# A two-layer diffusion trunk with grouped experts: the order in which experts are worked, and where the loops over their blocks end

## The chip, the core and the metric

The kernel runs on one core of one Trainium2 chip. The core has five engines: TensorE (PE in the profile, PEld for its weight loads), VectorE (DVE), ScalarE (ACT), GpSimd (POOL) and SyncE (SP), which here only issues transfers. Sixteen DMA engines move data between the device memory (HBM) and the on-chip memory. The metric is the device time of one execution in microseconds (us), the median of three runs.

## The reference, cut to what matters

The network has two layers: a Conformer convolution layer and a gated-linear-attention layer, each followed by a mixture of experts. Only the mixtures matter here. There are 32 experts in 4 groups of 8; each token picks a group, then the 2 best experts in it:

```
g_idx = jnp.argmax(hf @ wg + bg, axis=-1)
inner = (hf @ wr + br).reshape(t, MOE_GROUPS, MOE_PER_GROUP)     # of the chosen group
top_v, top_i = lax.top_k(inner, MOE_TOP_K)                       # 2 of 8
top_w = jax.nn.softmax(top_v, axis=-1) * g_w
expert = g_idx[:, None] * MOE_PER_GROUP + top_i
y = (jax.nn.silu(xb @ w1[e]) * (xb @ w3[e])) @ w2[e]             # xb: the tokens of expert e
out[token] += y * weight
```

The width is 1024, the inner width 512. The first mixture sees 1280 tokens (256 of the context, 1024 latent), the second 1024. Everything is float32: w1, w3 and w2 of one expert are 2 MB each, 6 MB together (6 transfers of 1024 KB), and 32 experts make 201 MB a layer.

## The kernel before, in words

Each layer ends in two phases. **route** (from line 1056) takes the router's scores and works out, on DVE, which expert has how many tokens, in which order the experts are worked, and where each token's row goes. An expert's tokens are cut into *blocks* of 32 (`BLK`), and `need` is its number of blocks, at least 1. `place` is an expert's place in the order, 0 to 31. The results are small tables: `plan.order` (the expert at each place), `plan.ends` (blocks up to and with that place), `plan.block` (the count of all blocks) and `plan.token` (the rows of each block).

**experts** (from line 1408) then works the blocks in that order. Its engines run five programs that meet at semaphores:

- SP (lines 1456 to 1483) streams the weights. `feed.w` holds four experts (`BUFS`). The first three places always belong to experts 0, 8 and 16, whose weights are asked for already during route. For each place x, SP waits until the weights of x have landed and says so (`pair_ready` for w1 and w3, line 1467; `back_ready` for w2, line 1469). Then, while x+3 exists, it waits until place x-1 has left its buffer (`pair_done`, `back_done`) and issues the load of place x+3: four transfers of 1024 KB for w1 and w3 (line 1026) and two for w2 (line 1034). All this is one program in order: what it says of place x+1 is said after the load of x+3 has been issued.
- PE (lines 1515 to 1577): per block, `in_product` (line 1533, 32 weight loads and 32 matmuls of 32 tokens by 2 x 128 columns), the turn of the next block's tokens (line 1520), `out_product` of the block before (line 1526) and the turn of its activations (line 1548). A new place waits for `pair_ready` before its first block.
- ACT and DVE: the activation, the gate product, and copying results out of PSUM. ACT stores a block's 128 KB of results. After all blocks each has a `tail` for the last block's results, which PE writes to `py_last`.
- POOL gathers the 128 KB of tokens of a block four blocks ahead and, in the second layer, starts the final gathers when the last results are stored.

ACT, DVE and POOL share the loop in `blocks` (lines 1437 to 1450): four blocks written out, then a loop of four blocks a turn whose number of turns is that of the greatest possible count `nb` (112 blocks in the first layer, 96 in the second), and each block inside stands under `If(k < count)`. PE's own loops end at `plan.ends`.

Of the kernel before, what the change touches and what calls it, by code (L numbers as in the profile page):

```python
# [10 lines left out]
ALU = mybir.AluOpType  # L11
AX = mybir.AxisListType
ds = bass.ds

P = 128
# [12 lines left out]
GROUPS, PER_GROUP, EXPERTS, FF, BLK = 4, 8, 32, 512, 32  # L28
EXPERT_ORDER = [g * PER_GROUP + e for e in range(PER_GROUP) for g in range(GROUPS)]
AHEAD_X = 4  # L30
MIDDLE = 18
ROUND = float(1 << 23)
LAT, CTX = 0, 1
SH1, SC1, G1, SH2, SC2, G2 = range(6)
# [13 lines left out]
class Phase:  # L48
# [9 lines left out]
    def sb(self, name, shape, dt=F32):  # L58
        return self.ctx.enter_context(self.nc.sbuf_tensor(f"{self.name}_{name}", shape, dt))
# [31 lines left out]
def chain(ph, eng, name):  # L91

    done = [0]

    def link(ins):
        done[0] += 1
        ins.then_inc(ph.sem(name), 1)
        eng.wait_ge(ph.sem(name), done[0])
    return link
# [956 lines left out]
def route(nc, d, layer, streams, plan, lg, ranks, feed):  # L1056
# [4 lines left out]
    nb = plan.blocks  # L1061
    width = GROUPS + EXPERTS
    with ExitStack() as ctx:
        ph = Phase(nc, ctx, f"route{layer}")
        s = ph.sem
        sb = feed.room()
# [21 lines left out]
        need = sb([P, EXPERTS])  # L1088
        key = sb([P, EXPERTS])
        place = sb([P, EXPERTS])  # L1090
        bend = sb([P, EXPERTS])
        first_of = sb([P, EXPERTS])
        last_of = sb([P, EXPERTS])
        versus = sb([P, EXPERTS, EXPERTS])
# [7 lines left out]
        with nc.Block() as block:  # L1102
# [33 lines left out]
            def _(dve):  # L1136
                link = chain(ph, dve, "step")
# [70 lines left out]
                link(dve.tensor_tensor(versus, other(key), this(key), ALU.is_gt))  # L1208
                link(dve.tensor_reduce(key, versus, AX.X, ALU.add))
                link(dve.tensor_scalar(place, key, float(feed.AHEAD), 0.0, ALU.subtract, ALU.max))  # L1210
                link(dve.tensor_scalar(bend, key, -4.0, float(4 * MIDDLE - 3), ALU.mult, ALU.add))
                link(dve.scalar_tensor_tensor(place, bend, 0.0, place, ALU.min, ALU.add))
                link(dve.tensor_tensor(place, place, key, ALU.add))

                link(dve.tensor_tensor(versus, other(place), this(place), ALU.is_lt))
                link(dve.tensor_tensor(versus, versus, other(need), ALU.mult))
# [13 lines left out]
                for j in range(2):  # L1230
# [13 lines left out]
                by_place = inner_rows[0:1, :, :]  # L1244
# [7 lines left out]
                link(dve.tensor_tensor(by_place.rearrange("p x (e g) -> p x e g", g=GROUPS),  # L1252
                                       versus[0:1, :, :].rearrange("p x (e g) -> p x e g", g=GROUPS),
                                       numbers.unsqueeze(1).to_broadcast([1, EXPERTS, PER_GROUP, GROUPS]), ALU.mult))
                link(dve.tensor_reduce(bend[0:1, :], by_place, AX.X, ALU.add))
                dve.tensor_copy(plan.order[:, :], bend[0:1, :]).then_inc(s("told"), 1)
                dve.wait_ge(s("told"), 4)
                dve.wait_ge(s("slots_done"), 1)

# [148 lines left out]
def experts(nc, d, layer, plan, feed, final_streams=None):  # L1408


    nb = plan.blocks
    UNROLL = 4
# [3 lines left out]
    with ExitStack() as ctx:  # L1416
        ph = Phase(nc, ctx, f"moe{layer}")
        s = ph.sem
# [6 lines left out]
        a = ph.sb("a", [P, P])  # L1425
        at = ph.sb("at", [P, P])
# [10 lines left out]
        def blocks(eng, body, tail=None):  # L1437

            count = eng.value_load(plan.block[0:1, 0:1], min_val=plan.fewest, max_val=nb)
            for k in range(UNROLL):
                body(k, 0, k)
            with eng.Fori(1, nb // UNROLL) as i:
                for p in range(UNROLL):
                    k = i * UNROLL + p
                    with eng.If(k < count):  # L1447
                        body(k, i, p)
            if tail:
                tail(count, eng.value_load(plan.block[0:1, 1:2], min_val=plan.fewest - 1, max_val=nb - 1))  # L1450
# [5 lines left out]
        with nc.Block() as block:  # L1456
# [31 lines left out]
            @block.gpsimd  # L1488
            def _(pool):
                def gather(k, p):  # L1490

                    pool.tensor_copy(idx[:, p:p + 1], plan.token[:, ds(k, 1)]).then_inc(s("idx_ready"), 1)  # L1492
                    pool.wait_ge(s("idx_ready"), k + 1)
                    pool.sem_inc(s("gathers"), 1)
                    pool.indirect_dma_start(xg[p][:, :], None, cut_rows, bass.IndirectOffsetOnAxis(idx[:, p:p + 1], 0))\  # L1495
                        .then_inc(s(f"gathered{p}"), 16)

                def body(k, i, p):

                    pool.wait_ge(s("x_here"), k + 1)  # L1500
                    gather(k + UNROLL, p)

                def finish(count, last):
                    for p in range(UNROLL):
                        pool.wait_ge(s(f"gathered{p}"), ((last + (2 * UNROLL - p)) >> 2) * 16)
                        pool.wait_ge(s(f"y_stored{p}"), ((last + (UNROLL - 1 - p)) >> 2) * 16)
                    pool.wait_ge(s("last_stored"), 16)
                    if final:
                        final.gather(pool)

                for k in range(UNROLL):
                    gather(k, k)
                blocks(pool, body, finish)
# [67 lines left out]
            def _(act):  # L1581
# [41 lines left out]

                take_x(0)
                blocks(act, body, tail)
                if final:
                    final.squares(act, ident[:, :])

            @block.vector
            def _(dve):  # L1630
# [33 lines left out]

                bring_x(0, 0, 0)
                blocks(dve, body, tail)
                if final:
                    final.rows(dve)
# [1241 lines left out]
def conv_layer(nc, d, rows):  # L2910

    with ExitStack() as ctx:
        plan = Plan(nc, ctx, 0, TILES)
        with ExitStack() as scores:
            lg = scores.enter_context(nc.sbuf_tensor("scores0", [P, TILES, GROUPS + EXPERTS], F32))
            ranks = scores.enter_context(nc.sbuf_tensor("ranks0", [P, EXPERTS], F32))
            with ExitStack() as conv:
                vt = conv.enter_context(nc.sbuf_tensor("taps_out", [P, KC, CONV_OUT], F32))
                vecs = conv.enter_context(nc.sbuf_tensor("channel_vectors", [P, KC, VEC_ROWS], F32))
                cs = conv.enter_context(nc.sbuf_tensor("silu_c", [P, KC, 2], F32))  # L2920
                raw = [conv.enter_context(nc.sbuf_tensor(f"taps_raw{b}", [P, KC, 2, P], F32)) for b in range(2)]
                ada_w = [conv.enter_context(nc.sbuf_tensor(f"taps_ada_w{h}", [P, KC // 2, N], F32))
                         for h in range(2)]
                w2_raw = [raw[b][:, h * 4:(h + 1) * 4, :, :].rearrange("p k h n -> p (k h n)")
                          for b in range(2) for h in range(2)]
                w2_raw += [ada_w[b][:, h * 2:(h + 1) * 2, :].rearrange("p k n -> p (k n)")
                           for b in range(2) for h in range(2)]
                with nc.sbuf_tensor("mod", [P, 2, 2, KC], F32, side="right") as mod:
                    front(nc, d, vt, vecs, cs, mod, raw)
                    ht = Split(nc, conv, "ht_conv", [P, KC, TOK])  # L2930
                    conv_taps(nc, d, ht, vt, vecs, cs, mod, raw, ada_w, w2_raw)
                conv_out(nc, d, vt, vecs, lg, ht, w2_raw, ranks)
            plan.hold(nc, scores, 0)
            feed = Feed(nc, scores, d, 0)
            route(nc, d, 0, STREAMS, plan, lg, ranks, feed)
            experts(nc, d, 0, plan, feed)
        ht_next = Split(nc, rows, "ht_next0", [P, KC, TOK], side="right")
        combine_values(nc, d, plan, ht_next)
    return ht_next


def gla_layer(nc, d, rows, ht):

    keep = ExitStack()
    with ExitStack() as ctx:
        qk = ctx.enter_context(nc.sbuf_tensor("qk", [P, 2 * HEADS, TOK], F32))
        cum = ctx.enter_context(nc.sbuf_tensor("cum", [P, 2, HEADS, TOK], F32))
        gla_keys(nc, d, ht, qk, cum)
        rows.close()
        w_raw = keep.enter_context(nc.sbuf_tensor("wo_w_raw", [P, EARLY, D], F32, side="right"))  # L2950
        gla_scan(nc, d, qk, cum, w_raw)
    with ExitStack() as ctx:
        plan = Plan(nc, ctx, 1, LAT_TILES)
        with ExitStack() as scores:
            lg = scores.enter_context(nc.sbuf_tensor("scores1", [P, LAT_TILES, GROUPS + EXPERTS], F32))
            ranks = scores.enter_context(nc.sbuf_tensor("ranks1", [P, EXPERTS], F32))
            gla_output(nc, d, lg, w_raw, ranks)
            keep.close()
            plan.hold(nc, scores, 1)
            feed = Feed(nc, scores, d, 1)  # L2960
            route(nc, d, 1, LAT_STREAMS, plan, lg, ranks, feed)
            experts(nc, d, 1, plan, feed, LAT_STREAMS)
# [92 lines left out]
```

## Time and profile before

| | us |
|---|---|
| median of 3 runs (2831.58 to 2833.03) | 2832.69 |
| the profiled execution, its own time | 2834.07 |
| its span | 2832.3 |
| PE busy | 2289.7 (81% of the span) |
| DVE busy | 1249.3 (44%) |
| ACT busy | 741.5 (26%) |
| POOL busy | 393.1 (14%) |
| DMA queue q1 (SP's) | 576.63 MB, 53.5% of 16 engines' span |

The span is what the profiler saw between the first and the last instruction; the execution's own time is 1.8 us longer. The experts of the first layer take from about 716 to 1430 us, those of the second from about 2227 to 2776 us. In the rows below a time is counted from the start of the span; `[0.80 <-SPq L1467]` behind an instruction says that its engine stood idle for 0.80 us before it and was released by line 1467 in SP's program. `SPq` rows are transfers being issued; their duration is the time that issuing took, not the transfer. `<-issue` is idle time in which the engine waited for nothing that the profile shows.

### The profile page before, as it was taken

Reading aid. Unit: us, or ns where it says so; the run is one execution under the profiler, and the core shown is the slowest. Engines: PE = TensorE matmul, PEld = TensorE weight load, DVE = VectorE, ACT = ScalarE, POOL = GpSimd, SP = SyncE. Lnnn points to the kernel's source line nnn. Section 1 sums busy time; section 2 is a strip of 40 time slices with the busy share of each in tenths; the row PEclk is TensorE's granted clock in tenths of the full one; section 3 lists DMA queues with packets and bytes.
Section 4 is the critical chain, followed back from the end, with each engine's and each line's share of the span. In section 5 each row is a group of like instructions: output and inputs, shape, how many; then the busy total and the mean of one; then the engine's idle time right before and its main releaser. Section 6 shows DMA issues by size and latency. Waiting matters only on the chain. (4 is left out here: it accounts for less than half of the span.)

```text
span 2832.3 us, 62953 instructions
## 1 busy us (share of the span) xinstructions
PE 2289.7 (81%) x24871; PEld 1539.8 (54%) x24872; DVE 1249.3 (44%) x2297; ACT 741.5 (26%) x1653; POOL 393.1 (14%) x592
## 2 busy tenths in 40 slices
PE   6888780895699999986619998979688399999895
PEld 3667670784355555543317885758577255554452
DVE  4779999666222222221135401328565422222224
ACT  5210101551121222211134312448532022111112
POOL 1000001000111111110012100025300111111112
PEclk9889895896899999988759999989898699999998
DMA  8374342235935557999955311014553999999994
GB/s 320 105 238 133 122 149 82 78 112 212 405 133 214 219 218 277 358 408 409 399 198 192 127 52 46 23 43 164 207 194 129 406 396 407 408 408 408 407 368 185
DMA packets 228379, 662.92 MB, mean 234 GB/s; under 512 B 26125, under 2 KB 56925, under 8 KB 228247
## 3 DMA queue, kind: packets, MB, share of 16 engines
q1 hardware_dynamic: 196028, 576.63, 53.5%
q0 software_dynamic: 19280, 56.60, 5.6%
q10 hardware_dynamic: 12940, 27.91, 3.0%
q8 instruction: 86, 1.41, 0.2%
q14 instruction: 45, 0.37, 0.0%
HBM read 583.52 MB, written 77.55 MB: 233 GB/s over the span
## 5 line engine op out<-in xcount | busy, mean ns | idle before, releaser
L1533 PE MATMUL moe_pg<-feed_w,moe_xt 128*32 128x256 f32 x11200 | 673.2, 394 | 107.3 <-SPq L1467 96.0
L1533 PEld LDWEIGHTS moe_pg<-feed_w,moe_xt 128*32 128x32 f32 x11200 | 357.5, 113 | 363.1 <-SPq L1467 100.1
L1526 PE MATMUL moe_py<-feed_w,moe_at 128*32 128x256 f32 x5536 | 334.8, 382 | 0.0
L1648 DVE TENSOR_TENSOR moe_a<-moe_sil,moe_pg 128x128 f32<-128x128 f32 x175 | 50.4, 288 | 644.3 <-ACT moe_sil L1606 644.3
L1640 DVE COPY moe_y<-moe_py 32x256 f32<-32x256 f32 x346 | 146.9, 424 | 283.6 <-PE moe_py L1526 278.2
L1606 ACT ACTIVATE moe_sil<-moe_pg 128x128 f32<-128x128 f32 x175 | 48.5, 277 | 701.6 <-PE moe_pg L1533 701.6
L1526 PEld LDWEIGHTS moe_py<-feed_w,moe_at 128*32 128x32 f32 x5536 | 161.6, 109 | 110.9
L1492 POOL COPY moe_idx<-plan_token 128x1 int32 (+1 forms) x183 | 33.5, 183 | 1273.0 <-DVE moe_x_rows L1636 872.3
L1592 ACT ACTIVATE moe_y<-moe_py 32x256 f32<-32x256 f32 x346 | 129.0, 373 | 279.1 <-PE moe_py L1526 274.9
L1495 POOL DMA_INDIRECT moe_xg<-scratch_experts_in,moe_idx x183 | 178.7, 977 | 144.1 <-POOL moe_idx L1492 144.1
L104 PE MATMUL taps_zg<-ht_conv_hi,taps_w_hi 128*128 128x512 f32 (+1 forms) x192 | 77.6, 404 | 66.3 <-DVE taps_w_lo L549 51.6
L104 PE MATMUL cv_acc<-cv_w_hi,ht_next_hi 128*128 128x512 f32 x288 | 117.6, 408 | 14.9 <-DVE ht_next_lo L1969 14.9
L1520 PE MATMUL moe_pxt<-moe_ident,moe_x_rows 128*128 128x128 f32 x354 | 89.3, 334 | 40.9 <-DMA moe_ident<-const_ident 40.9
L1520 PEld LDWEIGHTS moe_pxt<-moe_ident,moe_x_rows 128*128 128x128 f32 x354 | 55.3, 205 | 113.4 <-issue 72.0
L106 PE MATMUL cv_acc<-cv_w_hi,ht_next_lo 128*128 128x512 f32 x288 | 115.0, 399 | 0.0
L105 PE MATMUL cv_acc<-cv_w_lo,ht_next_hi 128*128 128x512 f32 x288 | 114.6, 398 | 0.0
L582 DVE SCALAR_TENSOR_TENSOR taps_acc<-taps_back,channel_vectors,taps_acc 128x649 f32<-128x649 f32 x120 | 107.2, 894 | 0.0
L570 DVE SCALAR_TENSOR_TENSOR taps_acc<-taps_u,taps_both,taps_acc 128x649 f32<-128x649 f32 x120 | 107.2, 893 | 0.0
L597 DVE SCALAR_TENSOR_TENSOR taps_acc<-taps_ahead,channel_vectors,taps_acc 128x649 f32<-128x649 f32 x112 | 92.0, 892 | 0.0
L521 ACT ACTIVATE taps_sg<-taps_zg,channel_vectors 128x512 f32<-128x512 f32 (+1 forms) x24 | 14.8, 615 | 269.2 <-PE taps_za L106 269.2
L104 PEld LDWEIGHTS taps_zg<-ht_conv_hi,taps_w_hi 128*128 128x128 f32 x192 | 43.6, 227 | 75.5 <-DVE taps_w_lo L549 53.4
L1587 ACT ACTIVATE moe_xt<-moe_pxt 128x256 f32<-128x256 f32 x177 | 67.5, 381 | 32.7 <-PE moe_pxt L1520 28.2
(356 smaller groups left out, 3922.7 us busy)
## 6 DMA issues: line engine op xcount, KB each, us to landing
feed_w<-in_moe_w SPq DMA_DIRECT2D x384, 1024.0 KB
taps_ada_w<-in_ada_w SPq DMA_DIRECT2D x40, 1024.0 KB, 7.0
scratch_experts_out<-moe_y ACTq DMA_DIRECT2D x175, 128.0 KB, 4.8
taps_raw<-in_conv_pw_w SPq DMA_DIRECT2D x20, 512.0 KB, 9.1
scan_v<-scratch_gla_values SPq DMA_DIRECT2D x20, 512.0 KB, 4.0
front_w<-in_ada_w SPq DMA_DIRECT2D x8, 1024.0 KB, 18.3
cv_raw<-in_gla_w_in SPq DMA_DIRECT2D x16, 512.0 KB
scratch_gla_out<-scan_o SPq DMA_DIRECT2D x16, 512.0 KB, 6.0
```

The lines of the kernel that those rows point to most:

```text
L104: pe.matmul(out, xh, wh, start=start, stop=False)
L105: pe.matmul(out, xh, wl, start=False, stop=False)
L106: return pe.matmul(out, xl, wh, start=False, stop=stop)
L570: dve.scalar_tensor_tensor(acc[0][:, :], src, tap, acc[0][:, :], ALU.mult, ALU.add)\
L582: dve.scalar_tensor_tensor(acc[1][:, :], src, tap, acc[1][:, :], ALU.mult, ALU.add)\
L597: dve.scalar_tensor_tensor(acc[q][:, :], src, tap, acc[q][:, :], ALU.mult, ALU.add)\
L1495: pool.indirect_dma_start(xg[p][:, :], None, cut_rows, bass.IndirectOffsetOnAxis(idx[:, p:p + 1], 0))\
L1520: last = pe.transpose(pxt[:, c * P:(c + 1) * P], x_rows[:, c::2], ident[:, :])
L1526: last = pe.matmul(out[j * BLK:(j + 1) * BLK, 0:CUT], at[:, c * BLK:(c + 1) * BLK], feed.back[:, buf, c, j * CUT:(j + 1) * CUT], start=c = ...
L1533: last = pe.matmul(pg[j * BLK:(j + 1) * BLK, 0:2 * P].rearrange("t (m n) -> t m n", m=2), xt[:, c % 2, (c // 2) * BLK:(c // 2 + 1) * BLK], ...
L1592: act.activation(y[b][:, j * CUT:(j + 1) * CUT], src[j * BLK:(j + 1) * BLK, 0:CUT], ACT.Copy)\
L1640: dve.tensor_copy(y[b][:, j * CUT:(j + 1) * CUT], src[j * BLK:(j + 1) * BLK, 0:CUT]).then_inc(s("y_far"), 1)
```

## The change

Two things. First, the order. In both versions the experts are ranked by their number of blocks (`key`: 0 for the most, with experts 0, 8, 16 fixed in front), and `place` is computed from the rank. Before, ranks 3 to 17 went to places 3, 5, 7, ..., 31 and ranks 31 down to 18 to places 4, 6, ..., 30. Now ranks 3 to 9 go to places 3, 7, ..., 27, ranks 10 to 16 to places 5, 9, ..., 29, ranks 17 to 23 to places 4, 8, ..., 28, ranks 24 to 30 to places 6, 10, ..., 30 and rank 31 to place 31. Second, the loop of `blocks` on ACT, DVE and POOL takes its number of turns from the count in a register.

```
-MIDDLE = 18
+LATER = ((7, -26.0), (14, -29.0), (21, -26.0), (28, -3.0))
...
-        bend = sb([P, EXPERTS])
+        bend = sb([P, len(LATER), EXPERTS])
+        numbered = sb([P, EXPERTS])
...
                 link(dve.tensor_scalar(place, key, float(feed.AHEAD), 0.0, ALU.subtract, ALU.max))
-                link(dve.tensor_scalar(bend, key, -4.0, float(4 * MIDDLE - 3), ALU.mult, ALU.add))
-                link(dve.scalar_tensor_tensor(place, bend, 0.0, place, ALU.min, ALU.add))
-                link(dve.tensor_tensor(place, place, key, ALU.add))
+                for i, (at, shift) in enumerate(LATER):
+                    link(dve.tensor_scalar(bend[:, i, :], place, float(at), shift, ALU.is_ge, ALU.mult))
+                link(dve.tensor_reduce(numbered, bend.rearrange("p i e -> p e i"), AX.X, ALU.add))
+                link(dve.scalar_tensor_tensor(place, place, 4.0, numbered, ALU.mult, ALU.add))
+                link(dve.scalar_tensor_tensor(place, key, float(feed.AHEAD), place, ALU.min, ALU.add))
...
-            with eng.Fori(1, nb // UNROLL) as i:
+            with eng.Fori(1, (count + (UNROLL - 1)) >> 2) as i:
+                i = nc.s_assert_within(i, 1, nb // UNROLL - 1,
+                                       skip_runtime_bounds_check_because="count is at most nb, a multiple of UNROLL")
```

The router of the reference, worked out on the reference's inputs, gives the blocks of each expert, and the rules above then give the blocks at each place, 0 to 31:

```
first layer, 96 blocks, before:  1 2 1 14 1 12 1 11 1 8 1 8 1 6 1 4 1 3 1 3 1 2 1 2 1 2 1 1 1 1 1 1
first layer, 96 blocks, now:     1 2 1 14 1 3 1 12 1 3 1 11 1 2 1 8 1 2 1 8 1 2 1 6 1 1 1 4 1 1 1 1
second layer, 79 blocks, before: 2 3 2 4 1 3 2 3 2 3 2 3 2 3 2 3 2 3 2 3 2 3 2 3 2 3 2 3 2 3 2 2
second layer, 79 blocks, now:    2 3 2 4 2 3 2 3 2 3 2 3 2 3 2 3 2 3 2 3 2 3 2 3 2 3 2 3 2 3 2 1
```

On DVE, in route, these are the instructions around the changed ones, before. `feed_w` is the buffer in which route keeps its small arrays; 128x32 is one value per expert, 128x1024 a comparison of every expert with every other:

```order
L1208 TENSOR_TENSOR feed_w<-feed_w 128x1024
L1209 TENSOR_REDUCE feed_w<-feed_w 128x32
L1210 TENSOR_SCALAR feed_w<-feed_w 128x32
L1211 TENSOR_SCALAR feed_w<-feed_w 128x32
L1212 SCALAR_TENSOR_TENSOR feed_w<-feed_w 128x32
L1213 TENSOR_TENSOR feed_w<-feed_w 128x32
L1215 TENSOR_TENSOR feed_w<-feed_w 128x1024
```

And now, in the same place:

```order
L1209 TENSOR_TENSOR feed_w<-feed_w 128x1024
L1210 TENSOR_REDUCE feed_w<-feed_w 128x32
L1211 TENSOR_SCALAR feed_w<-feed_w 128x32
L1213 TENSOR_SCALAR feed_w<-feed_w 128x32 x4
L1214 TENSOR_REDUCE feed_w<-feed_w 128x32
L1215 SCALAR_TENSOR_TENSOR feed_w<-feed_w 128x32
L1216 SCALAR_TENSOR_TENSOR feed_w<-feed_w 128x32
L1218 TENSOR_TENSOR feed_w<-feed_w 128x1024
```

Three small instructions between the rank and the comparison of places have become seven; each waits for the one before it. Nothing else in route moves.

On ACT, at the end of the loop of `blocks` in the first layer, before (the last row of one block's branch, the loop's own step, and the load of the count for the tail):

```order
L1447 UNCONDITIONAL_BRANCH
L1444 REGISTER_ALU
L1444 COMPARE_AND_BRANCH
L1450 TENSOR_LOAD plan_block
L1450 ISA x2
```

And now:

```order
L1452 UNCONDITIONAL_BRANCH
L1447 ISA
L1447 COMPARE_AND_BRANCH
L1455 TENSOR_LOAD plan_block
L1455 ISA x2
```

The instructions are as many as before; the loop's step has become another register instruction, and the comparison is against a register. DVE and POOL have the same rows. No instruction of PE or SP moves: the new order of the experts reaches them through the tables.

## Rows read from the trace of the kernel before

**Rows 1.** The page's groups: ACT's activation, one per block.
```profile
L1606 ACT ACTIVATE moe_sil<-moe_pg 128x128 f32<-128x128 f32 x175 | 48.5, 277 | 701.6 <-PE moe_pg L1533 701.6
```
**Rows 2.** Stretches: busy us of each engine, clock of PE, DMA share, GB/s.
```profile
716.00:1421.00 705.00, 612.06 (x9474) 329.54 (x9474) 154.72 (x476) 127.92 (x382) 115.94 (x200) 0.93 0.78 301
860.00:932.00 72.00, 72.00 (x1151) 39.14 (x1142) 17.92 (x55) 14.44 (x44) 12.74 (x22) 0.98 0.44 157
1156.00:1164.00 8.00, 8.00 (x136) 4.29 (x128) 1.63 (x5) 1.30 (x4) 2.14 (x3) 1.00 0.21 59
1166.00:1218.00 52.00, 50.40 (x813) 27.45 (x809) 13.54 (x42) 11.23 (x34) 9.26 (x16) 1.00 1.02 407
1180.00:1400.00 220.00, 156.06 (x2277) 81.68 (x2269) 38.42 (x119) 31.49 (x93) 27.80 (x48) 0.85 1.03 408
2330.00:2740.00 410.00, 385.34 (x6047) 208.57 (x6041) 99.36 (x305) 80.63 (x244) 70.63 (x122) 0.98 1.03 408
```
**Rows 3.** PE's waits in 716 to 1430 us, then in 2227 to 2780 us.
```profile
PE moe_pg L1533 <- SPq L1467: 70.5, 17, 10.0
...
PE moe_pg L1533 <- SPq L1467: 25.4, 10, 5.3
```
**Rows 4.** PE in order of time, first layer: first products of some blocks.
```profile
849.12 3.66 PE L1533 MATMUL moe_pg<-feed_w,moe_xt 128*32 128x256 f32 x64
...
858.96 1.51 PE L1533 MATMUL moe_pg<-feed_w,moe_xt 128*32 128x256 f32 x12 [3.63 <-issue]
...
1166.49 3.66 PE L1533 MATMUL moe_pg<-feed_w,moe_xt 128*32 128x256 f32 x64
...
1173.51 3.66 PE L1533 MATMUL moe_pg<-feed_w,moe_xt 128*32 128x256 f32 x64 [0.80 <-SPq L1467]
...
1179.66 3.66 PE L1533 MATMUL moe_pg<-feed_w,moe_xt 128*32 128x256 f32 x64
...
1232.97 5.35 PE L1533 MATMUL moe_pg<-feed_w,moe_xt 128*32 128x256 f32 x64 [3.13 <-SPq L1467]
...
1415.05 3.66 PE L1533 MATMUL moe_pg<-feed_w,moe_xt 128*32 128x256 f32 x64
```
**Rows 5.** SP in order of time: loads of weights being issued, first layer.
```profile
847.07 2.26 SPq L1026 DMA_DIRECT2D feed_w<-in_moe_w  x4
...
1164.42 2.31 SPq L1026 DMA_DIRECT2D feed_w<-in_moe_w  x4
...
1211.20 7.21 SPq L1034 DMA_DIRECT2D feed_w<-in_moe_w  x2
...
1234.30 12.37 SPq L1026 DMA_DIRECT2D feed_w<-in_moe_w  x4
```
**Rows 6.** PE, second layer: the first block of place 29.
```profile
2726.32 3.66 PE L1533 MATMUL moe_pg<-feed_w,moe_xt 128*32 128x256 f32 x64
```
**Rows 7.** The end of the first layer's blocks, all engines.
```profile
1422.43 1.93 PE L1526 MATMUL moe_py_last<-feed_w,moe_at 128*32 128x256 f32 x32 [1.16 <-DVE moe_at L1657]
1428.31 0.88 DVE L1640 COPY moe_y<-moe_py_last 32x256 f32<-32x256 f32 x2 [5.93 <-issue]
1428.42 0.77 ACT L1592 ACTIVATE moe_y<-moe_py_last 32x256 f32<-32x256 f32 x2 [6.50 <-issue]
```
**Rows 8.** The end of the second layer's blocks, all engines.
```profile
2770.57 1.93 PE L1526 MATMUL moe_py_last<-feed_w,moe_at 128*32 128x256 f32 x32 [1.16 <-DVE moe_at L1657]
2776.24 0.77 ACT L1592 ACTIVATE moe_y<-moe_py_last 32x256 f32<-32x256 f32 x2 [6.16 <-issue]
```
**Rows 9.** ACT's branches in the loop: ns least/median/greatest.
```profile
L1447 ACTq COMPARE_BRANCH  x200: 34/34/53, 761.0 to 2775.2; - x100
```
**Rows 10.** DVE in route, in order of time.
```profile
693.63 0.18 DVE L1210 TENSOR_SCALAR feed_w<-feed_w 128x32 f32<-128x32 f32 x1
693.85 0.18 DVE L1211 TENSOR_SCALAR feed_w<-feed_w 128x32 f32<-128x32 f32 x1
...
699.35 0.82 DVE L1221 TENSOR_REDUCE feed_w<-feed_w 128x20 f32<-128x640 f32 x1
```

More of the change, by code:

```diff
@@ L1254, in _ @@
                                        numbers.unsqueeze(1).to_broadcast([1, EXPERTS, PER_GROUP, GROUPS]), ALU.mult))
-                link(dve.tensor_reduce(bend[0:1, :], by_place, AX.X, ALU.add))
-                dve.tensor_copy(plan.order[:, :], bend[0:1, :]).then_inc(s("told"), 1)
+                link(dve.tensor_reduce(numbered[0:1, :], by_place, AX.X, ALU.add))
+                dve.tensor_copy(plan.order[:, :], numbered[0:1, :]).then_inc(s("told"), 1)
                 dve.wait_ge(s("told"), 4)
```

## The prediction, written before the changed kernel ran

> **What bounds the kernel now.** I read the page first, then the stretches, then PE's waits, then the order of time on PE and SP. The reader should see five things.
>
> 1. There are 96 + 79 = 175 blocks by the reference's router, and 175 activations [rows 1].
> 2. Of PE's idle time in the experts, 70.5 us in the first layer and 25.4 in the second are waits for `pair_ready` (line 1467) [rows 3]: weights, or word of them, are late.
> 3. The first layer is lopsided [rows 2]. Early, with places of 12 and 8 blocks, PE is never idle and the DMA engines are 44% busy (157 GB/s): four buffers are full and nothing may be loaded. Late, with places of 1 to 3 blocks, they carry 408 GB/s without a gap for 220 us, and PE is busy for 156. Work that could overlap stands one after the other.
> 4. The second layer carries 408 GB/s for 410 us: the transfers bound it.
> 5. SP's own program can be the late one. It must issue the load of place x+2 before it tells of place x. From 1164.42 to 1211.20 + 7.21 = 1218.4 it issues four whole loads, 24 transfers or 25.2 MB [rows 5], with the DMA nearly empty before (59 GB/s) and full after (407) [rows 2]. In 52 us at 407 less the blocks' own 43 GB/s (2 x 131 KB per 6.15 us), 19.0 MB have moved. So about 6.1 MB, one load, is all that stands issued and undone; beyond that the issuing stalls (12.37 us for four transfers late on [rows 5]), and word of weights already landed is late with it.
>
> **The unit prices.** A block is 6.15 us (1173.51 to 1179.66 [rows 4]). A place with one block takes 7.02 (1166.49 to 1173.51), 0.87 more, since SP tells of the next place only after issuing a load that waits for this block. After a wait of 3 us PE's first product takes 5.35 us instead of 3.66, 1.7 more [rows 4]: PE has fallen to the lower of its two clocks, 1.2 GHz, and climbs back to 2.4 under way. The mean granted clock of 0.85 in the starved stretch, against 1.00 in a dense one [rows 2], is the same thing. A load is 6.29 MB, at 364 GB/s 17.3 us.
>
> **The new order, first layer.** Up to place 5 the numbers of blocks are the same as before, so its start at 858.96 [rows 4] stays (the code's 3.63 us of issue before it too). From there I walk the places. After a heavy place three light ones follow, of 3 to 5 blocks; the next heavy place can start when PE is there and SP has said so. Before saying so SP must issue three loads, and the first of them cannot go before the heavy place's last product. Price: four loads took 54.0 us with an empty DMA, less one of 17.3 is 36.7; SP begins 2.05 before the next place's first block (847.07 against 849.12 [rows 5, 4]), so 34.7 us after the heavy place ends. While PE waits some 8 us the blocks' traffic is gone (43 GB/s x 8 us = 0.34 MB, 0.9 us): 33.8. The light places themselves take 5 x 6.15 + 2 x 0.87 = 32.5, 4 x 6.15 + 1.7 = 26.3 or 3 x 6.15 + 2.6 = 21.1. So:
>
> - place 7: 858.96 + 4 x 6.15 + 0.9 + 1.7 = 886.1; its 12 blocks end at 959.9
> - place 11: 959.9 + 34.7 = 994.6; 11 blocks end at 1062.3
> - place 15: + 33.8 = 1096.1; 8 blocks, slow first, end at 1147.0
> - place 19: + 33.8 = 1180.8; end 1231.7
> - place 23: + 33.8 = 1265.5; 6 blocks end at 1304.1
> - place 27: + 33.8 = 1337.9; 4 blocks end at 1364.2
> - places 28 to 31: 4 x 6.15 + 3 x 0.87 = 27.2, end 1391.4.
>
> The last load is issued at about 1362 with half a load in front of it and its w1 and w3 need 11.5 us: about 1382, before PE gets to place 31 at 1385. Before, the last block started at 1415.05 [rows 4] and ended at 1421.2. The gain is 29.8 us. Bounds: if SP is allowed 0.5 MB more in flight, four waits shrink by 1.4 each (-35); if a half MB less and each wait breeds another slow product, -24. The larger gain has the wider bound, so I take 31, a little beyond the walk. What is late next: still line 1467, at places 15, 19, 23, 27, some 7 to 13 us each.
>
> **The new order, second layer.** Loads bound it, and the bytes are the same. From place 29 on (2726.32 [rows 6]) PE never waits: its 3 + 2 + 2 blocks are now 3 + 2 + 1, 6.15 us less. Place 4 has two blocks instead of one, so loads 8 and 9 are issued up to 6 us later, where the DMA is just short of running dry; that may cost 0 to 3, and I take 0.
>
> **DVE in route.** Three small instructions go, seven come [rows 10]: one is 0.22 us from start to start (693.63 to 693.85), six at 0.22 and a reduction of 128 values, between 0.22 and the 0.82 of one of 640 [rows 10], less three at 0.22: +0.88 to +1.5. It is nearest to the small ones: 0.95 a layer. DVE is the last engine of route, and all wait for it at the phase's end. In the first layer it is on the path in full. In the second the first three loads cover the transfers, but PE starts that much later: 0 to 0.95, take 0.95.
>
> **The loop's end.** Before, ACT and DVE step through four turns of untaken branches after the last block of each layer: DVE idles 5.93 us and ACT 6.50 [rows 7], while PE's last product ends at 1422.43 + 1.93 = 1424.36 and ACT starts its copy only at 1428.42. With the turns gone both stand ready (0.25 us behind PE): 1424.6, a gain of 3.8. In the second layer 2776.24 against 2772.50 + 0.25: 3.5 [rows 8], and POOL's final gathers wait for the store behind this copy. If POOL's phase end in the first layer doesn't move with it, 3.8 are lost. The dearer loop step is a few tens of ns a turn, under PE's products, where ACT waits 3 us a block: nothing.
>
> The Trainium skill (Advanced Engine Details and Errata, Control Flow Timing) gives a compare-and-branch about 108 ns. Four turns of five branches would then be 2.2 us, over before PE's last product, and nothing would be gained here. The trace disagrees: a branch itself is 34 ns [rows 9], yet the engines idle 5.93 and 6.50 us; the register work around it costs more than the branch.
>
> The Trainium skill (DMA: Bandwidth & Descriptors, Specifications) puts the memory's limit for a core at about 358 GB/s. By it three loads would be accepted some 6 us later at each of four places, and the sum would be about 24 us poorer. The rows show 407 and 408 GB/s here [rows 2], so it is not used.
>
> **The sum.** Against the profiled execution's own time, 2834.07 (span 2832.3 and 1.8 around it): -31 + 0.95 - 3.8 - 6.15 + 0.95 - 3.5 = -42.5, so 2791.5. The median of the runs is 1.4 lower, 2832.69: 2790. What a measurement of this kernel can tell from no change is about 0.2%, 5.7 us.
>
> **Rivals.**
>
> *Word comes at landing.* If the limit of 6 MB is an effect of the starved stretch and not SP's rule, only bytes and blocks count. PE then ends place 23 at 858.96 + 66 x 6.15 + 9 x 0.87 + 1.7 = 1274; loads 27 to 31 follow at 17.3 each, to 1360, and PE ends some 8 later: 1368, a gain of 53 instead of 31: 2768. For it: early loads of one or two places are issued without delay. Against it: the 54.0 us. Chance 0.10.
>
> *The loop gives nothing* (a register bound costs as much, or POOL's end stands still): 7.3 us less gain, 2797. For it: nothing in the trace shows a loop on a register here, except PE's, which have no cheap skip. Against: the idle time ends with the branches. Chance 0.08.
>
> *Slower: a burst of four.* If, when a heavy place ends, the load issued at its start is not done, SP must get four loads accepted in the light places, not three: 54.0 - 2.05 = 52 instead of 33.8, 18 us at each of five places (11, 15, 19, 23, 27), 91 more: +48, 2881. It decides from the point where the heavy place is shorter than 6.1 + 6.3 MB at 364 GB/s, 34 us or 5.5 blocks. Places 7 to 23 have 12, 11, 8, 8 and 6 blocks, all over, the last barely. Place 27 is under, but only light places follow. Chance 0.03.
>
> *The order isn't as said.* The formula checks by hand: rank 3 gives 0 + 3, rank 10 gives 28 - 26 + 3 = 5, rank 31 gives 112 - 84 + 3 = 31. If ties or counts differ on the chip the shape remains. Chance 0.02, within 0.2%.
>
> **How the numbers follow.** The forecast has 0.77 and its own range, 2784 to 2798. The range of 8 in 10 reaches into the first two rivals: 2776 to 2802. Faster by over 0.2%: 0.77 + 0.10 + 0.08 = 0.95; within: 0.02; slower: 0.03.
>
> **What would show it.** Right: PE's waits on line 1467 in the first layer near 50 us, in lumps before places 11 to 27; place 7 starting near 886; SP's issues stalling inside each light group; the DMA engines' share more even, near 0.82 over the phase; the idle before the last copies under 2.5 us; the second layer's last place with one block. Wrong: the heavy places starting without a wait (first rival), or waiting over 15 us each (third).

## The result and the profile after

The changed kernel takes 2784.2 us, the median of four runs (2778.7 to 2786.6), against 2832.3 of the kernel before beside it: a ratio of 0.983, 95% interval 0.981 to 0.984. In a later series it took 2783.8 (2778.0 to 2784.6). The forecast was 2790, with 2784 to 2798 as its own range and 2776 to 2802 as that of 8 in 10.

The profiled execution is the shortest of its four, 2778.7; that of before, 2834.1, lies 1.8 above its median. Between those two traces lie 55.3 us, between the medians 48.1. A second trace of the changed kernel (an execution of 2783.7, span 2781.9) shows what belongs to the change and what to one execution.

The stretches, as in [rows 2] (busy us of PE, PEld, DVE, ACT, POOL, then PE's clock, the DMA share and GB/s):

```profile
700.00:1383.00 683.00, 615.38 (x9634) 334.82 (x9634) 170.38 (x506) 135.90 (x384) 116.42 (x200) 0.95 0.82 320
860.00:932.00 72.00, 71.04 (x1135) 38.80 (x1131) 18.21 (x56) 16.11 (x46) 12.79 (x22) 1.00 0.83 323
1180.00:1340.00 160.00, 143.92 (x2204) 76.94 (x2206) 36.15 (x111) 31.47 (x90) 25.58 (x44) 0.94 0.94 369
2330.00:2700.00 370.00, 348.00 (x5440) 187.62 (x5433) 89.29 (x274) 76.83 (x218) 63.96 (x110) 0.97 1.03 408
```

The second line is the same 72 us in which the DMA engines were 44% busy before; they now carry 323 GB/s there. The third lies in the stretch that was starved. The kernel before had this in the same 160 us:

```profile
1180.00:1340.00 160.00, 123.05 (x1826) 65.01 (x1822) 30.27 (x94) 24.58 (x73) 22.00 (x38) 0.87 1.03 408
```

PE is now busy for 90% of it and not for 77%, at a granted clock of 0.94 and not 0.87. The second layer looks as before.

PE's waits for `pair_ready` in the two layers, which answer to [rows 3] (total, times, longest):

```profile
PE moe_pg L1538 <- SPq L1472: 37.3, 14, 6.6
...
PE moe_pg L1538 <- SPq L1472: 22.0, 8, 4.6
```

70.5 us have become 37.3, less than the 50 that the forecast named as its sign. They stand in lumps ahead of the heavy places from 15 on, as forecast, but also before places 26 and 29; before place 11, where a lump was forecast too, PE waits only 0.80 us. PE in order of time at places 7, 15, 19, 23 and 27 (start, duration, idle time ahead):

```profile
884.15 2.15 PE L1538 MATMUL moe_pg<-feed_w,moe_xt 128*32 128x256 f32 x36 [0.96 <-SPq L1472]
...
1090.25 2.36 PE L1538 MATMUL moe_pg<-feed_w,moe_xt 128*32 128x256 f32 x20 [6.36 <-SPq L1472]
...
1174.35 1.93 PE L1538 MATMUL moe_pg<-feed_w,moe_xt 128*32 128x256 f32 x16 [6.59 <-SPq L1472]
...
1256.66 1.93 PE L1538 MATMUL moe_pg<-feed_w,moe_xt 128*32 128x256 f32 x16 [5.88 <-SPq L1472]
...
1325.79 2.79 PE L1538 MATMUL moe_pg<-feed_w,moe_xt 128*32 128x256 f32 x24 [4.48 <-SPq L1472]
```

What SP does meanwhile, from the end of heavy place 11 on (transfers of one expert: four of line 1026, two of line 1034):

```profile
1056.08 2.40 SPq L1026 DMA_DIRECT2D feed_w<-in_moe_w  x4
1064.37 0.89 SPq L1034 DMA_DIRECT2D feed_w<-in_moe_w  x2
1066.72 2.01 SPq L1026 DMA_DIRECT2D feed_w<-in_moe_w  x4
1071.39 4.59 SPq L1034 DMA_DIRECT2D feed_w<-in_moe_w  x2
1077.43 9.47 SPq L1026 DMA_DIRECT2D feed_w<-in_moe_w  x4
1087.00 3.13 SPq L1034 DMA_DIRECT2D feed_w<-in_moe_w  x2
1091.58 11.69 SPq L1026 DMA_DIRECT2D feed_w<-in_moe_w  x4
1103.36 5.37 SPq L1034 DMA_DIRECT2D feed_w<-in_moe_w  x2
```

The third load is issued at 1087.00 + 3.13 = 1090.13, and PE starts place 15 at 1090.25, 0.12 us after SP is through with issuing.

The end of the first layer's blocks, against [rows 7]:

```profile
1383.77 1.93 PE L1531 MATMUL moe_py_last<-feed_w,moe_at 128*32 128x256 f32 x32 [1.16 <-DVE moe_at L1662]
1385.90 0.77 ACT L1597 ACTIVATE moe_y<-moe_py_last 32x256 f32<-32x256 f32 x2 [2.63 <-PE moe_py_last L1531]
1385.93 0.87 DVE L1645 COPY moe_y<-moe_py_last 32x256 f32<-32x256 f32 x2 [2.21 <-PE moe_py_last L1531]
```

Both engines now wait for PE, not PE's result for them: the copy comes 0.2 us after the product's end and not 4.1 us. (ACT's idle time of 2.63 us is a little above the 2.5 named as a sign; all of it is now a wait for PE.) And DVE in route, against [rows 10]:

```profile
692.41 0.18 DVE L1211 TENSOR_SCALAR feed_w<-feed_w 128x32 f32<-128x32 f32 x1
692.63 0.83 DVE L1213 TENSOR_SCALAR feed_w<-feed_w 128x32 f32<-128x32 f32 x4
693.50 0.37 DVE L1214 TENSOR_REDUCE feed_w<-feed_w 128x32 f32<-128x128 f32 x1
693.90 0.19 DVE L1215 SCALAR_TENSOR_TENSOR feed_w<-feed_w 128x32 f32<-128x32 f32 x1
694.13 0.19 DVE L1216 SCALAR_TENSOR_TENSOR feed_w<-feed_w 128x32 f32<-128x32 f32 x1
694.36 1.23 DVE L1218 TENSOR_TENSOR feed_w<-feed_w 128x1024 f32<-128x1024 f32 x1
```

From line 1211 to the comparison at 1218 are 1.95 us. The three instructions that stood there before took 0.89, so the cost is 1.06 a layer.

All traces by stage, in us. A layer runs from its first block's start to its last block's end; "between" from there to the second layer's first block; "tail" from the last block to the end of the span.

| trace | layer 1 | between | layer 2 | tail | span | median of the runs |
|---|---|---|---|---|---|---|
| before | 690.5 | 824.1 | 524.1 | 62.9 | 2832.3 | 2832.3 to 2835.2 |
| changed | 653.2 | 820.1 | 518.3 | 55.9 | 2776.9 | 2784.2 |
| changed, again | 653.4 | 822.9 | 518.9 | 56.1 | 2781.9 | 2783.8 |
| order_only | 654.2 | 825.9 | 518.9 | 59.6 | 2790.2 | 2790.6 |
| loop_only | 690.0 | 820.9 | 523.9 | 56.6 | 2820.8 | 2823.6 |
| direct | 631.3 | 820.9 | 502.2 | 59.2 | 2744.5 | 2746.0 |
| direct_old | 686.0 | 820.7 | 509.9 | 57.4 | 2803.5 | 2805.3 |
| rising | 658.3 | 821.9 | 521.9 | 56.2 | 2786.4 | 2787.5 |
| rising_direct | 604.7 | 824.0 | 501.5 | 59.3 | 2719.3 | 2718.3 |
| falling | 737.4 | 823.6 | 527.2 | 56.9 | 2873.1 | 2877.2 |
| shifted | 662.8 | 821.0 | 519.5 | 56.4 | 2795.3 | 2796.9 |
| last_heavy | 665.8 | 818.8 | 523.2 | 59.2 | 2796.5 | 2803.2 |

"Between" scatters by 5 us among kernels with the new loop (818.8 to 824.0), about as much as executions of one kernel differ by. The layers are the sharp measure: twice the same kernel gives 653.2 and 653.4.

### The profile page after: what moved, and what is told of

Its sections match the earlier page's. It is cut to its first block and busy times, and to the rows that moved or that the text cites. A ratio compares the mean times of both kernels' runs of the same rounds, so it can differ in the third digit from the quotient of the medians.

```text
span 2776.9 us, 62721 instructions
## 1 busy us (share of the span) xinstructions
PE 2283.0 (82%) x24871; PEld 1537.4 (55%) x24872; DVE 1250.6 (45%) x2305; ACT 755.9 (27%) x1653; POOL 394.7 (14%) x592
## 5 line engine op out<-in xcount | busy, mean ns | idle before, releaser
L1538 PE MATMUL moe_pg<-feed_w,moe_xt 128*32 128x256 f32 x11200 | 670.3, 393 | 67.8 <-SPq L1472 59.3
L1497 POOL COPY moe_idx<-plan_token 128x1 int32 (+1 forms) x183 | 33.8, 185 | 1227.8 <-DVE moe_x_rows L1641 825.7
L104 PE MATMUL taps_zg<-ht_conv_hi,taps_w_hi 128*128 128x512 f32 (+1 forms) x192 | 77.2, 402 | 65.4 <-DVE taps_w_lo L549 50.6
L1525 PEld LDWEIGHTS moe_pxt<-moe_ident,moe_x_rows 128*128 128x128 f32 x354 | 55.3, 205 | 110.6 <-issue 72.0
```

The lines of the kernel that those rows point to most:

```text
L104: pe.matmul(out, xh, wh, start=start, stop=False)
L1525: last = pe.transpose(pxt[:, c * P:(c + 1) * P], x_rows[:, c::2], ident[:, :])
L1538: last = pe.matmul(pg[j * BLK:(j + 1) * BLK, 0:2 * P].rearrange("t (m n) -> t m n", m=2), xt[:, c % 2, (c // 2) * BLK:(c // 2 + 1) * BLK], ...
```

## The experiments

### One part at a time: order_only, loop_only

order_only keeps the new order and has the old bound back; loop_only is the kernel before with

```
-            with eng.Fori(1, nb // UNROLL) as i:
+            with eng.Fori(1, (count + (UNROLL - 1)) >> 2) as i:
```

> The changed kernel with the old bound of the loop over blocks: all 24 of its rounds are walked again, in both layers; the new order of the experts stays. My theory (the order is worth about 41 us, the loop about 7.3 us, and the two add): 2832.3 - 41 = 2791 us, and between the last block and the last copy 20.3 us of layer 1 come back as before. Rival A (the loop is worth nothing, because the pool's drain ends the phase anyway): same time as the changed kernel, 2784. Rival B (the loop's end is worth more than the two ends of phases, since the last phase of the changed kernel was also 3.3 us shorter): 2794 to 2796.

> The kernel before with the loop over blocks ending at the count, the old order of experts kept. My theory: 2832.3 - 3.8 - 3.5 = 2825 us; the wait of PE for pair_ready in layer 1 stays near 70 us in 17 lumps. Rival A (nothing, the ends are hidden): 2832. Rival B (the 3.3 us of the last phase belong to the loop's end): 2821.5.

Measured: 2790.6 us (2787.0 to 2792.0, five runs; 0.985 of before, 0.983 to 0.986) and 2823.6 (2819.6 to 2825.9, seven runs; 0.997, 0.996 to 0.998). The order alone gives 42.1 us, the loop alone 9.1, or 6.8 on top of the order; together 48.9. They add within the scatter. In order_only the idle time ahead of the last copies is back, and in loop_only it is shorter and all of it a wait for PE:

```profile
1387.00 1.93 PE L1529 MATMUL moe_py_last<-feed_w,moe_at 128*32 128x256 f32 x32 [1.16 <-DVE moe_at L1660]
1392.88 0.87 DVE L1643 COPY moe_y<-moe_py_last 32x256 f32<-32x256 f32 x2 [5.93 <-issue]
1393.00 0.77 ACT L1595 ACTIVATE moe_y<-moe_py_last 32x256 f32<-32x256 f32 x2 [6.49 <-issue]
```

```profile
1420.59 1.93 PE L1528 MATMUL moe_py_last<-feed_w,moe_at 128*32 128x256 f32 x32 [1.16 <-DVE moe_at L1659]
1422.72 0.77 ACT L1594 ACTIVATE moe_y<-moe_py_last 32x256 f32<-32x256 f32 x2 [2.63 <-PE moe_py_last L1528]
1422.75 0.87 DVE L1642 COPY moe_y<-moe_py_last 32x256 f32<-32x256 f32 x2 [2.21 <-PE moe_py_last L1528]
```

From the last block to the next phase's first transfer order_only has the 20.3 us of the kernel before, and loop_only 16.5 (order_only's expectation puts these 20.3 us before the last copy; they end at the next phase's start). So the rival that the loop gives nothing is out. Rival B, that the loop's end is worth some 3 us more, isn't excluded by loop_only's time, halfway between the two. Against it stand order_only, whose five runs all lie below the 2794 that B asks for, and the traces: the tails of order_only and of the second trace of the changed kernel differ by 3.5 us, the predicted step and nothing more.

### The changed kernel again: after_again

> The changed kernel once more, for a second trace and more times. If the 3.3 us by which its last phase was shorter than before's belong to the change, the last copy of layer 2 stands again 52.6 us before the end of the span; if they are scatter between executions, it stands at 52.6 to 56 us, and the execution's time moves with it. Time: 2784 us (2779 to 2787).

2783.8 us (four runs), 0.982 of before (0.981 to 0.984). The tail is 56.1 us as in the first trace, and order_only, whose loop is the old one, has 59.6 and not before's 62.9. So the further 3.3 us between the first two traces are not the old loop's alone (order_only has that loop and lacks them), nor the old order's alone (loop_only has that order and a tail of 56.6). That leaves the one profiled execution of before, or the two together; with a single trace of that kernel this isn't shown.

### Who is late, the weights or the word: direct, direct_old

direct is the changed kernel with PE waiting for the load's own semaphore; direct_old is loop_only with the same edit:

```
-                    sp.sem_inc(s("pair_ready"), 1)
...
-                    sp.sem_inc(s("back_ready"), 1)
...
-                    pe.wait_ge(s("pair_ready"), x + 1)
+                    pe.wait_ge(feed.sem(f"pair_loaded{b}"), turn * 64)
```

(and the waits for `back_ready` likewise).

> The changed kernel, but TensorE waits for the arrival of each expert's weights on the semaphore of the load itself, and no longer for SyncE to pass it on (SyncE's own waits for its loads stay). My theory: SyncE, stalled in the issue of its next transfers while 6 to 7 MB are outstanding, tells of a load that has landed late; with the wait on the load the blocks of layer 1 end about 28 us earlier, those of layer 2 about 17 us earlier: 2784 - 45 = 2739 us (2730 to 2752). Rival (the queue's bandwidth and not the telling sets the light places): no change, 2780 to 2786.

> The order of the kernel before, with the loop over blocks ending at the count, and TensorE waiting for each expert's weights on the semaphore of the load itself. My theory: in the old order the light places of the second half wait for bandwidth (about 17 us of transfer for 7 to 13 us of blocks), not for SyncE's word, so the direct wait gives only about 9 us in layer 1 and 14 us in layer 2: 2824 - 23 + 3 = 2804 us (2796 to 2810); the new order is then worth 2804 - 2746 = 58 us with direct waits, against about 40 with told ones. Rival (the direct wait is worth the same 40 us in any order, the two changes simply add): 2786 us.

Measured: direct 2746.0 us (2745.5 to 2750.2), 0.970 of before (0.968 to 0.971), 37.9 less than the changed kernel. In its trace no place from 9 to 26 of layer 1 waits at all; even the 0.87 us after each one-block place is gone. The weights had been there each time. At place 15, before which the changed kernel had idled 6.36 us, PE goes straight on from the block before:

```profile
1077.06 3.66 PE L1536 MATMUL moe_pg<-feed_w,moe_xt 128*32 128x256 f32 x64
1083.20 3.66 PE L1536 MATMUL moe_pg<-feed_w,moe_xt 128*32 128x256 f32 x64
```

The sum was 7 us too good: layer 1 gave 22 and not 28 (places 30 and 31 now wait 8.8 and 7.0 us for the data and then start slowly, about 10 us each), and the tail is 3.1 longer. The new order told by SP had 37.3 us of waits in layer 1; this is what is left of them:

```profile
PE moe_pg L1536 <- DMA feed_w<-in_moe_w: 20.8, 4, 8.8
```

direct_old: 2805.3 us (2802.1 to 2809.0), as expected, and not 2786: its layer 1 waits 65.4 us for the data itself:

```profile
PE moe_pg L1533 <- DMA feed_w<-in_moe_w: 65.4, 10, 10.9
```

The four kernels form a square. With SP's word the order is worth 2823.6 - 2783.8 = 39.8 us, with direct waits 2805.3 - 2746.0 = 59.3; the direct wait is worth 18.3 in the old order and 37.9 in the new. In the old order the late places lack bandwidth, in the new one mostly the word. The changed kernel had turned one limit into the other, and a third of the order's possible gain stayed there.

### Which order: rising, rising_direct, falling, last_heavy

rising and rising_direct add four DVE instructions that mirror ranks 3 to 9, so that places 3, 7, ... 27 have 4, 6, 8, 8, 11, 12, 14 blocks. falling takes the rank itself as the place. last_heavy changes only the table:

```
-LATER = ((7, -26.0), (14, -29.0), (21, -26.0), (28, -3.0))
+LATER = ((8, -30.0), (15, -29.0), (22, -26.0))
```

> The changed kernel with the seven heaviest of places 3, 7, ... 27 in rising order (the lightest of them at place 3, the heaviest at place 27); SyncE tells of the loads as in the changed kernel. By my place-by-place sum: layer 1 +4 us (the first heavy place of 4 blocks is over before the queue has caught up, the later ones are all long), layer 2 -4, routing +1: 2785 us (2775 to 2795). Rival (what counts is only that heavy and light alternate evenly, the order of the heavy ones is free): 2784 us, the same; rival B (the heavy ones are needed early, to gain a lead for the rest): over 2800 us.

> Rising order of the heavy places and TensorE waiting on the loads themselves. By my place-by-place sum, corrected by nothing: layer 1 25 us and layer 2 4 us less than in the changed order with direct waits, because heavy places late give the queue work for the light ones at the end: 2746 - 29 = 2717 us (2710 to 2735). Rival (the order of the heavy places is free): 2746.

> The changed kernel with the places simply in falling order of blocks (all heavy experts first, the 1-block experts last, places 0 to 2 as before), which the spread order avoids. By my place-by-place sum: while the heavy experts run the queue is idle behind four full buffers, and about 16 light experts then cost a load's time each (17.3 us for 7 us of blocks): layer 1 +90 us, layer 2 +11 us: 2784 + 101 = 2885 us (2860 to 2910), slower than the kernel before. Rival (blocks, not loads, bound the layer): within 10 us of 2784.

> The changed kernel with a table of three rules and not four: eight experts on every fourth place with the last of them at place 31, so that the last place of layer 1 has 3 blocks and not 1, and some light places one block less. Theory (place-by-place sum): the blocks are as many, but those at place 31 come after the last wait and cover no load, while the light places ahead of it lose them: layer 1 longer by 13 us, layer 2 the same: 2797 us (2789 to 2801). Rival (only the even spread counts): 2784 us (2781 to 2787).

rising took 2787.5 us (2786.8 to 2788.2): layer 1 is 4.9 longer, as summed, layer 2 is 3.0 longer where 4 less was summed. rising_direct took 2718.3 us (2714.6 to 2721.1), 0.959 of before (0.958 to 0.961), the fastest kernel here. Its layer 1, 604.7 us, is 96 x 6.15 = 590 and 14 more, with no wait for weights left (the second layer still has four, of 0.5 to 3.9 us); all that is named for the first layer's products is this:

```profile
PE moe_pg L1540 <- issue: 9.9, 5, 3.7
PE moe_pg L1540 <- ACT moe_xt L1594: 0.5, 1, 0.5
```

So the rival that the order of the heavy places is free holds within 4 us while SP tells, and is wrong by 28 us once PE doesn't depend on its word: with the longest places late, the light ones at the end find their loads done: places 28 to 31, which cost direct three waits, start without one.

falling took 2877.2 us (2874.9 to 2878.9), 1.016 of before (1.014 to 1.018): layer 1 gave +84 where +90 was summed. Its two halves (columns as above):

```profile
760.00:1200.00 440.00, 439.32 (x7073) 240.28 (x7077) 115.82 (x356) 100.34 (x286) 82.24 (x142) 1.00 0.54 198
1200.00:1465.00 265.00, 153.62 (x2012) 76.31 (x2007) 32.74 (x101) 28.53 (x81) 22.02 (x38) 0.76 1.01 400
```

The same blocks and bytes, apart in time: first PE is full and the queue half empty, then the other way round, at a clock of 0.76. The same change with another table would have been slower than before.

last_heavy took 2803.2 us (2797.3 to 2807.6; 0.989 of before, 0.987 to 0.991), 19 more than the changed kernel (the series had before 2.5 us higher) and 2 above the range expected. Layer 1 is 12.5 longer (13 summed). Layer 2 is 4.4 longer where nothing was summed: its last places have 2, 1 and 3 blocks and not 3, 2 and 1, and place 30, with the one block, now waits and starts slowly (5.35 us and not 3.66):

```profile
2710.99 5.35 PE L1538 MATMUL moe_pg<-feed_w,moe_xt 128*32 128x256 f32 x64 [3.05 <-SPq L1472]
```

Blocks at the last place cover no load. That supports the term of 6.15 us for the second layer, from the other side.

### Why the waits were shorter than priced: shifted

The prediction priced a light group at 33.8 us; the trace has 31.9, 32.1, 31.4 and 30.7 before places 15, 19, 23 and 27. In SP's rows above the pair of transfers at 1087.00 takes 3.13 us, and the next pair, at 1103.36, with the queue as full, takes 5.37. One by one, around the word for place 15:

```profile
1087.00 2.62 SPq L1034 DMA_DIRECT2D feed_w<-in_moe_w  x1
...
1089.71 0.42 SPq L1034 DMA_DIRECT2D feed_w<-in_moe_w  x1
1091.58 4.00 SPq L1026 DMA_DIRECT2D feed_w<-in_moe_w  x1
```

One transfer is taken at once, and the next pays for it. I counted through every trace with the order of SP's transfers: where the queue is full, the transfer whose number in layer 1 is 3 modulo 8 takes 0.4 us (once 1.8), most of the others 2.2 to 2.8 in the middle, and the one behind it often about 4; in layer 2 it is the one that is 1 modulo 8, at 0.4 to 0.7 on average in all but falling. (Numbers start at 0 in each layer.) A light group with its heavy place is four loads, 24 transfers, three times eight, so the quick one comes at the same spot in every group: right ahead of the word. shifted puts two transfers ahead of layer 1's loads:

```
+                if feed.layer == 0:
+                    for h in range(2):
+                        sp.dma_start(feed.pair[:, 2, 0, h * KC // 2:(h + 1) * KC // 2, :]
...
+                                     ).then_inc(s("spent"), 16)
```

> The changed kernel with two more transfers of 1 MB (a piece of one expert's weights, overwritten later) in SyncE's queue ahead of the first expert of layer 1, so that every later transfer of weights has a number higher by two. In all traces so far a stalled transfer is taken in 0.4 us with 6.2 to 7.1 MB outstanding when its number in the layer is 3 modulo 8, and at about 5.9 MB otherwise; in the changed order 3 modulo 8 falls on the last transfer of the third load of each light group, which stands right ahead of the word for the heavy place. Theory A (the position in the queue decides): the quick one moves to residue 1, the last transfer of the load before the word is taken about 2.2 us later, and places 15, 19, 23 and 27 start that much later each: layer 1 longer by 9 us, layer 2 within 3 us, 2793 us (2789 to 2797). Theory B (the last transfer of a load, or the one before a pause, is taken early wherever it stands): no change, 2784 us (2781 to 2787).

Measured 2796.9 us (2795.1 to 2800.5; 0.987 of before, 0.985 to 0.989), 13.1 more than the changed kernel in another series, in which before had a median 2.5 lower. The stages say it better. Layer 1 is 9.5 longer (9 expected); the rest is its start, 5 to 6 us later behind the two added transfers, which the expectation had left out. The quick transfer has moved by two, into the four of line 1026:

```profile
1092.43 2.61 SPq L1026 DMA_DIRECT2D feed_w<-in_moe_w  x1
...
1095.14 0.42 SPq L1026 DMA_DIRECT2D feed_w<-in_moe_w  x1
1095.66 5.96 SPq L1034 DMA_DIRECT2D feed_w<-in_moe_w  x1
1101.71 2.35 SPq L1034 DMA_DIRECT2D feed_w<-in_moe_w  x1
```

and SP is through at 1104.1, when PE starts place 15:

```profile
1104.17 2.36 PE L1546 MATMUL moe_pg<-feed_w,moe_xt 128*32 128x256 f32 x20 [8.67 <-SPq L1480]
```

The light groups now cost 34.2, 34.5, 34.2 and 33.3 us: the forecast's 33.8. In layer 2 the quick transfer has moved too, from 1 to 7 modulo 8 of that layer's loads, which is again 1 when all 386 transfers are numbered through. Theory A holds, and B, that the last transfer of a load is taken early wherever it stands, is out.

## Why the prediction came out right, point by point

| step | predicted | in the traces |
|---|---|---|
| layer 1, order | -31 (walk -29.8; -35 to -24) | -37.3, -37.1; order_only -36.3 |
| DVE in route | +0.95 a layer | +1.06 |
| end of the loop, layer 1 | -3.8 | -3.8 (last block to the next phase's first DMA, 20.3 to 16.5) |
| layer 2, order | -6.15, place 4 at 0 (to +3) | -5.8, -5.2 |
| end of the loop, layer 2 | -3.5 | -3.5 (tails of order_only and of the changed kernel's second trace) |
| sum | -42.5 | medians -48.1 and -48.9 |

**The mechanism** was right in each step that carries the sum. Early and late work of the first layer had stood one after the other, and now overlap ([rows 2] against the stretches above). Starts of places, forecast and measured: 7 at 886.1 and 884.2, 11 at 994.6 and 990.7, 15 at 1096.1 and 1090.3, 19 at 1180.8 and 1174.4, 23 at 1265.5 and 1256.7, 27 at 1337.9 and 1325.8, end of the blocks 1391.4 and 1382.5.

**The term that was off** is "Price: four loads took 54.0 us ... 33.8" of the first layer: the true price is 31.5 on average. Place 11, priced at 34.7, took 32.5, which is no more than what its five light blocks take on PE (5 x 6.15 + 2 x 0.87): the three loads ahead of SP's word cost nothing there. Place 27 came 12.1 us early (1.4 of them because that execution started early). The price rested on four loads elsewhere in the trace, where the quick transfer lay inside the group and not at its end; shifted brings it back. The walk also lacked the waits before place 26, inside the last group, and before place 29; from place 27 on the layer was 3.2 us dearer than summed. So its end came 8.9 us before the walk's and not 12.1. The bound "if SP is allowed 0.5 MB more in flight, four waits shrink by 1.4 each" had the right place and too small a size: the transfer is 1.05 MB, and the waits shrank by 2.3.

**The loop.** All as forecast, and POOL's phase end moved with it, which was left open. order_only and loop_only bracket the predicted 7.3: 6.8 and 9.1. The 108 ns for a compare-and-branch of the Trainium skill (Advanced Engine Details and Errata, Control Flow Timing) would have had the turns over before PE's last product; the idle time of 5.93 and 6.49 us in order_only, which in loop_only is only the wait for PE's product, decides against it for these loops.

**The rivals.** "Word comes at landing" is false for the changed kernel, as its own wait for SP at 1090.13 shows. As a kernel of its own it is direct, with 2746 and not 2768: its layer 1 ended at 1362.0 where the rival had 1368, and layer 2, where the rival had no gain, gave 16.7. "The loop gives nothing" fell by loop_only. "A burst of four" didn't happen; the way to be slower that the runs do show is falling, an order with all heavy places first.

The forecast missed the median by 6 us, and its term for the first layer alone (-31 against -37.3) accounts for that. That the median still lies inside the forecast's own range, 0.2 us above its lower end, is luck; the wider bound of -35 for this term was too narrow as well.

## What to carry to other kernels

When a phase streams weights into a few buffers and its steps use them for unequal times, spread the long steps evenly: the average of busy shares hides that one half starves the transfers and the other the products. Put the shortest step very last, where nothing is left to load. Let the consumer wait on the transfer itself, and only then put the longest steps late: that was worth 28 us here with direct waits, and with SP's word it cost 4. As to the word: an engine that both issues transfers and passes on their completion is late with the word as soon as issuing stalls, here for 38 us after the reorder and 18 before it.

## What was new about the hardware

- Issuing stalls when about 6 MB of this queue's transfers are outstanding (by the queue's packets in the late first layer of before, changed, direct and shifted: 5.3 to 6.4 MB at the end of a stalled issue, 6.6 to 7.2 at the end of a quick one), but not evenly: of eight transfers of 1 MB in a row one is taken in 0.4 us, and the next often takes 4 or more (4.00 in the changed kernel's rows, 5.96 in shifted's). Which one it is goes by the count of transfers issued before, and it moved by two when two were added. What in the queue has that period wasn't tested; nor whether it counts transfers, bytes or descriptors, which are proportional here.
- Runs of one kernel in one series differ by 1 to 11 us, while a layer of blocks repeated within 0.2 and 0.6 us in the two traces of the changed kernel. What a single trace has in its tail is not yet the kernel's.
- With direct waits the tail is 0.5 to 3 us longer (57.4, 59.2, 59.3 against 55.9 to 56.9), though last_heavy has 59.2 too. Why stays open.
